# Row statistics as 128x4 columns spread over PSUM by TensorE, norm pieces in PSUM, the sums of squares on GpSimd, the last FFN pair ahead of the last two down products, and one key slab for two

## The chip, the cores and the metric

The kernel runs on one NeuronCore of one Trainium2 chip. The metric is device microseconds of one execution, the median of several runs. The core has five engines with queues of their own: PE (TensorE, matmuls; PEld is its weight load), DVE (VectorE), ACT (ScalarE), POOL (GpSimd) and SP (SyncE, which here only issues DMAs). They meet only through semaphores.

## The reference, cut to what matters

Two blocks in a row over one stream x of 1024 positions by 1024 channels, all in float32.

```
# first block
h = rmsnorm(x) ; z = h @ w_in                       # 1024 x 2560
y_a = a_bg * dwconv3(a_cg * a_h)
u   = dwconv31(b_val * sigmoid(b_gate)) + bias
y_b = silu(layernorm(u))                            # mean and variance over 512 channels
x   = x + [y_a, y_b] @ w_out
h = rmsnorm(x)
x = x + (silu(dwconv3(h @ w_gate)) * (h @ w_up)) @ w_down      # D_FF = 2816 = 22 tiles of 128
x = rmsnorm(x, norm_final_g)
# second block
h = rmsnorm(x) * (1 + scale) + shift ; pooling mixer, 4 groups ; x = x + gate * (... @ a_w_out)
hk = rmsnorm(x) * (1 + scale_kv) + shift_kv ; k, v = hk @ w_kv # 2 kv heads of 64: k is 128 columns, v 128
h = rmsnorm(x) * (1 + scale) + shift ; q, z = h @ b_w_in ; windowed attention with sinks
x = x + gate * (o * silu(z)) @ b_w_out
out = rmsnorm(x, final_g)
```

## The kernel before, in words

**Layout.** Channels lie on the 128 partitions and positions on the free axis: the stream `X` is 128 x 8 x 1024. Every product is in two parts, a high one rounded to fp32r and a low rest: w_hi\*x_hi + w_hi\*x_lo + w_lo\*x_hi, three matmuls of 128x512 (lines 449 to 451, and 502 to 504 in `gated_pair`). A weight **slab** is 128x1024. SP brings it to one of two `w_raw` buffers (L326), ACT rounds it to `w_hi` (L807, `weight_hi`), POOL makes `w_lo` (L356, `lower`), and the next slab but one can only be loaded when POOL is done with that buffer (`slab_ready`). Six pairs of `w_hi`/`w_lo` places are reused in a planned order (`SLAB_PLACE`, `slab_ends`, `refill_after`).

**Order.** Each engine's program is written out by hand; nothing is scheduled by a planner. PE takes *slab tiles* (24 matmuls: one 128-column slab against one half of the positions) and *down jobs* (16 tiles of 6 matmuls, whose results DVE adds to `X`: L1375, L1280, L1282, L1688), rotating through PSUM banks 0 to 3. A tile waits until the reader of its bank, four tiles back, is done (`freed`).

**Norms.** There are seven: MIX, FFN, FIN1 and POOL (both on the stream after the FFN), KV and ATT (one statistic for both), FIN2. Behind each of the 16 adds of the last down job ACT squares the new piece of `X` into one of two buffers (L828), and the squares are summed over the 8 channel tiles of a half into `T[2]`: on DVE (`add_square`, L1209) for FFN, KV and the second half of FIN2, on POOL (`sums`, L380) for FIN1 and the first half of FIN2. For POOL, DVE sums squares that carry FIN1's gain (L1523) and joins the two sums (L1529). A float32 matmul with a 128x128 matrix of ones (`stat`, L466) sums over partitions and leaves 128 equal rows of 512. ACT takes the root (L851), DVE the reciprocal (`rstd`, L1198), both on 128x512. Then for each of 16 pieces DVE multiplies (`scaled`, L1222, from `X` and `T[2]`, both in SBUF, into a piece in SBUF), ACT rounds it into `norm_hi` (`hi`, L859 or L861) and DVE subtracts (`low`, L1231 or L1233). PE follows piece by piece in `gated_pair`, 6 matmuls for each. `apply_early` puts the first pieces behind the last adds of the down job, `apply` does the rest.

**The layernorm** of the first block sits inside the four output down jobs. In front of tile 4 of the first one PE sums the four conv results of each half with eight matmuls of ones (L552); DVE subtracts the mean, ACT squares, POOL sums (L406), PE sums again (L558), ACT takes the root, DVE the reciprocal (L1388, 128x512), DVE scales (L1395), ACT applies SiLU and rounds, DVE subtracts (L1400). Those steps are placed behind single adds by `behind_first` and `behind_second`.

**FFN.** Eleven pairs: pair 0 in `gated_pair`, ten loop turns with two pairs and one down job of two y tiles each, and after the loop the pair for y tile 21 and the last down job. `ffn_y` has two places.

**Keys.** Slabs 150 and 151 each hold the 64 key columns of one kv head twice, slab 152 the values. `gated_pair` computes both key slabs, then two slab tiles give the values (in the KV norm's `norm_hi`), and only then may ACT write the ATT norm over it.

## Time and profile before

| | us |
|---|---|
| median of 3 runs (2251.2 to 2256.27) | 2255.36 |
| the profiled execution, its own time | 2253.53 |
| its span, first to last instruction | 2251.6 |
| PE busy in the span | 2125.0 (94%) |
| DVE busy | 1340.2 (60%) |
| ACT busy | 657.6 (29%) |
| POOL busy | 612.6 (27%) |
| mean granted TensorE clock | 0.98 |

The page gives busy time by engine, the span in 40 slices, the chain that ended last and the costliest groups. PE's busy time is that of overlapping matmuls, so it tells that PE had work and not that it was at its peak. What ended an idle time stands behind an arrow: `[8.46 <-DVE norm_lo L1233]` says that the engine had stood still for 8.46 us and that the DVE instruction of line 1233 released it.

### The profile page before, as it was taken

The numbers are of one execution on the slowest core, as the hardware profiler recorded it, in microseconds if no ns is written. First come the engines' busy times: TensorE is split into PE (matmuls) and PEld (weight loads), VectorE is DVE, ScalarE is ACT, GpSimd is POOL, SyncE is SP. The second block draws the span as 40 slices with busy tenths as digits, with TensorE's granted clock in tenths as the row PEclk, the third lists the DMA queues.
The fourth block names the chain that finished last, engine by engine and source line by source line (L and its number), as shares of the span: only waits on it lengthen the run. The fifth ranks groups of instructions, "written<-read, shape, count | busy, mean of one in ns | idle before, by whom it ended". The sixth has DMA issues, their size and how long they took to land.

```text
span 2251.6 us, 24476 instructions
## 1 busy us (share of the span) xinstructions
PE 2125.0 (94%) x9252; PEld 1704.7 (76%) x9252; DVE 1340.2 (60%) x1652; ACT 657.6 (29%) x1150; POOL 612.6 (27%) x280
## 2 busy tenths in 40 slices
PE   6999988899999999999889999999999789779996
PEld 4788766788888888888668888888888568557885
DVE  6998878455545556554785452463553831995557
ACT  4222333321222212121442122121221432785112
POOL 2223420321212222121431132121221123443622
PEclk9999999999999999999989999999999999999998
DMA  4131110422323231232011121111111111010202
GB/s 143 57 96 46 56 38 0 178 65 85 112 93 112 94 111 50 99 105 100 19 56 38 38 70 43 38 56 47 47 56 31 45 47 38 10 29 10 75 10 75
DMA packets 42951, 141.70 MB, mean 63 GB/s; under 512 B 3568, under 2 KB 7808, under 8 KB 42880
## 3 DMA queue, kind: packets, MB, share of 16 engines
q1 hardware_dynamic: 29984, 101.38, 14.2%
q10 hardware_dynamic: 12896, 39.36, 4.6%
q8 instruction: 47, 0.77, 0.1%
q14 instruction: 24, 0.20, 0.0%
HBM read 136.50 MB, written 7.36 MB: 64 GB/s over the span
## 4 chain that ended last, share of the span: by engine, by line
PE 81%; DVE 14%; issue 2%; ACT 1%; POOL 1%; DMA 1%; DVEq 0%; ACTq 0%; SPq 0%; POOLq 0%
PE psum L449 26%; PE psum L451 26%; PE psum L450 26%; DVE temp L1222 2%; DVE temp L1198 1%; DVE top L1635 1%; DVE w_lo L1653 1%; DVE probs L1632 1%; DVE norm_lo L1233 1%; PE psum L459 1%; DVE temp L1209 1%; DVE norm_lo L1231 1%; POOL w_lo L356 1%; DMA w_raw<-in_slabs 0%; DVE stream L1269 0%
## 5 line engine op out<-in xcount | busy, mean ns | idle before, releaser
L356 POOL TENSOR_TENSOR w_lo<-w_raw,w_hi 128x1024 fp32r<-128x1024 f32 x177 | 451.4, 2568 | 1347.5 <-ACT w_hi L807 1345.8
L449 PE MATMUL psum<-norm_hi,w_hi 128*128 128x512 f32 x1712 | 670.3, 392 | 19.0 <-ACT keys L884 6.5
L450 PE MATMUL psum<-norm_lo,w_hi 128*128 128x512 f32 x1712 | 668.6, 391 | 0.0
L451 PE MATMUL psum<-norm_hi,w_lo 128*128 128x512 f32 x1712 | 668.5, 390 | 0.0
L449 PEld LDWEIGHTS psum<-norm_hi,w_hi 128*128 128x128 f32 x1712 | 323.1, 189 | 88.4 <-issue 19.4
L451 PEld LDWEIGHTS psum<-norm_hi,w_lo 128*128 128x128 f32 x1712 | 322.8, 189 | 67.8
L450 PEld LDWEIGHTS psum<-norm_lo,w_hi 128*128 128x128 f32 x1712 | 323.0, 189 | 67.2
L884 ACT ACTIVATE temp<-psum 128x512 f32<-128x512 f32 x160 | 93.8, 598 | 460.7 <-PE psum L451 445.1
L1282 DVE SCALAR_TENSOR_TENSOR stream<-psum,mods,stream 128x512 f32<-128x512 f32 x160 | 119.7, 750 | 170.8 <-PE psum L451 170.6
L807 ACT CAST w_hi<-w_raw 128x1024 fp32r<-128x1024 f32 x158 | 158.8, 1046 | 146.0 <-DMA w_raw<-in_slabs 81.3
L1280 DVE TENSOR_TENSOR stream<-psum,stream 128x512 f32<-128x512 f32 x176 | 118.2, 688 | 79.4 <-PE psum L451 79.1
L1334 DVE SCALAR_TENSOR_TENSOR psum<-glu,vec,psum 128x1024 f32<-128x1024 f32 x116 | 149.6, 1290 | 3.9
L449 PE MATMUL psum<-ffn_y_hi,w_hi 128*128 128x512 f32 x352 | 141.4, 402 | 1.5 <-DVE stream L1280 1.4
L450 PE MATMUL psum<-ffn_y_lo,w_hi 128*128 128x512 f32 x352 | 139.2, 396 | 0.0
L451 PE MATMUL psum<-ffn_y_hi,w_lo 128*128 128x512 f32 x352 | 139.2, 395 | 0.0
L1469 DVE CUSTOM_DVE_ANT_0 ada_raw<-ada_raw,c_act 128x1024 f32<-128x1024 f32 x64 | 117.3, 1891 | 1.6 <-ACT c_act L985 1.6
L1442 DVE TENSOR_SCALAR psum<-temp,vec 128x1024 f32<-128x1024 f32 x22 | 28.3, 1288 | 142.7 <-ACT temp L884 142.4
L502 PE MATMUL psum<-norm_hi,w_hi 128*128 128x512 f32 x160 | 71.0, 444 | 38.8 <-DVE norm_lo L1233 18.2
L1564 DVE TENSOR_TENSOR temp<-temp 128x1024 f32<-128x1024 f32 x40 | 73.7, 1843 | 49.5 <-ACT temp L884 48.4
L449 PE MATMUL psum<-pool_y_hi,w_hi 128*128 128x512 f32 x256 | 101.5, 397 | 0.0
L451 PE MATMUL psum<-pool_y_hi,w_lo 128*128 128x512 f32 x256 | 101.1, 395 | 0.0
L450 PE MATMUL psum<-pool_y_lo,w_hi 128*128 128x512 f32 x256 | 101.1, 395 | 0.0
(171 smaller groups left out, 2865.2 us busy)
## 6 DMA issues: line engine op xcount, KB each, us to landing
w_raw<-in_slabs SPq DMA_DIRECT2D x177, 512.0 KB, 3.5
ada_raw<-in_ada ACTq DMA_DIRECT2D x10, 3072.0 KB, 12.2
stream<-in_x SPq DMA_DIRECT2D x8, 512.0 KB, 8.7
out<-stream SPq DMA_DIRECT2D x8, 512.0 KB, 2.8
skew_scratch<-row_scratch ACTq DMA_DIRECT2D x1, 3072.0 KB, 18.0
ada_raw<-in_ada ACTq DMA_DIRECT2D x1, 2048.0 KB, 9.8
bias<-skew_scratch ACTq DMA_DIRECT2D x4, 512.0 KB, 3.7
c_act<-in_c ACTq DMA_DIRECT2D x1, 512.0 KB, 11.4
```

What stands on the lines that cost most here:

```text
L356: nc.gpsimd.tensor_tensor(WL[place][:, :], RAW[at % 2][:, :], WH[place][:, :].bitcast(f32), ALU.subtract).then_inc(slab_ready, 1)
L449: nc.tensor.matmul(dst, wh, xh, start=n == 0, stop=False)
L450: nc.tensor.matmul(dst, wh, xl, start=False, stop=False)
L451: last = nc.tensor.matmul(dst, wl, xh, start=False, stop=n == len(terms) - 1)
L502: nc.tensor.matmul(dst, wh, xh, start=k == 0, stop=False)
L807: nc.scalar.copy(WH[place][:, :], RAW[at % 2][:, :]).then_inc(w_hi_done, 1)
L884: nc.scalar.activation(dst, bank[b], func, scale=scale).then_inc(act_read, 1)
L1280: ins = nc.vector.tensor_tensor(part, src, part, ALU.add)
L1282: ins = nc.vector.scalar_tensor_tensor(part, src, mods[:, gate + e:gate + e + 1], part, ALU.mult, ALU.add)
L1334: step(nc.vector.scalar_tensor_tensor(ACC, window, w, ACC, ALU.mult, ALU.add))
L1469: ins = nc.vector.tensor_tensor_reduce(out=ADA[:, n, :], in0=ADA[:, n, :], in1=c_act[:, :], scale=1.0, scalar=0.0, op0=ALU.mult, op1=ALU.a ...
L1564: step(nc.vector.tensor_tensor(body(T[dst]), body(T[src]), T[src][:, 16 - width:16 - width + S], ALU.add))
```

## The change

- **Statistics.** `stat` no longer makes 128 equal rows. `columns` takes the summed squares as the stationary operand, 128 positions at a time, and a single column of ones as the moving one: 4 matmuls leave 128x4. ACT's root and DVE's reciprocal work on 128x4 (`stat_col`). `across` then multiplies each column, broadcast over 128, by the identity: 4 matmuls put the 128 equal rows of 512 into a PSUM bank (`spread`). `stat` stands in front of tile 11 of the down job (before: 10, for POOL 13), `spread` in front of tile 13. For the second half they stand at steps 4 and 7 of `gated_pair`. MIX stays as it was.
- **Pieces.** `scaled` reads the spread statistic from bank 4 or 5 and writes its piece to bank 6 or 7, from which ACT and DVE read it.
- **Sums.** FFN, KV and FIN2 (all but the very last square) are summed on POOL. For POOL, DVE multiplies FIN1's plain squares by the squared gain and accumulates in PSUM (`add_gained`); ACT's second square of each piece goes, and `join_sums` becomes a second term of the column matmuls.
- **Layernorm.** POOL adds up the four conv results of each half in `T[2]` (6 adds, counted by `ln_pre`) behind its third weight slab of the last in-projection, and PE sums with one matmul of ones for each half in front of tile 4. Variance, root, reciprocal and spread go the new way, and DVE's scale and low steps are laid one behind each add.
- **FFN.** `ffn_y` has three places. The pair for y tile 21 comes straight behind the last turn's two pairs, ahead of the last two down jobs; SP loads the slabs in that order.
- **Keys.** Slab 150 holds the 64 key columns of both heads, brought by two DMAs of 64 columns in a row; slab 151 the values. `gated_pair` computes both, the two separate value tiles are gone, ACT makes the doubled keys with four copies of 64 partitions for each half, and writes the ATT norm of a half as soon as it has read that half.
- **End.** 14 of the 16 final pieces are normed by DVE (before 13), the other 2 by ACT and POOL; POOL's factor is a second spread in bank 7, copied to SBUF by ACT.

The diff, cut to its core:

```diff
-SLAB_PLACE += [0, 1] + [4]
-SLAB_PLACE += [2 * p + h for p in (1, 0, 2, 0, 2, 0, 1, 2, 0, 1, 2, 0) for h in (0, 1)]
+SLAB_PLACE += [0, 1]
+SLAB_PLACE += [2 * p + h for p in (1, 2, 0, 2, 0, 2, 1, 0, 2, 1, 0, 2) for h in (0, 1)]
...
         def piece(n, m):
-            return body(T[1], m % 2) if n != ATT and m < 8 else slot(m)
+            if n != MIX:
+                return bank[6 + m % 2]
+            return body(T[1], m % 2) if m < 8 else slot(m)
...
# sync
+            load_slabs(2, LAST_GATE)
+            load_slabs(LAST_GATE, LAST_GATE + 2, 2)
+            load_slabs(LAST_GATE + 2, LAST_GATE + 4, -2)
+            load_slabs(LAST_GATE + 4, ATT_SLAB)
+            sp.wait_ge(slab_ready, ATT_SLAB - 1)
+            for n in range(2):
+                if n:
+                    sp.wait_ge(keys_ready, 16)
+                keys = slab_in[ATT_SLAB + n, :, :].rearrange("p (k c) -> p k c", k=KT)[:, :, HD * n:HD * n + HD]
...
# gpsimd
                 lows(14 + 3 * j, 17 + 3 * j)
+                if j == MT - 1:
+                    gp.wait_ge(taps_done, MT)
+                    for n in range(1, MT):
+                        gp.wait_ge(conv_done, n + 1)
+                        for half in range(2):
+                            part = body(T[2], half)
+                            if n > 1:
+                                gp.wait_ge(ln_pre, 2 * n - 3 + half)
+                            nc.gpsimd.tensor_tensor(part, body(UB[4], half) if n == 1 else part,
+                                                    body(UB[(n + 4) % 5], half), ALU.add).then_inc(ln_pre, 1)
...
-            lows(26, FFN_SLAB + 6)
+            lows(26, FFN_SLAB + 2)
+            sums(FFN)
+            lows(FFN_SLAB + 2, FFN_SLAB + 6)
...
-            lows(ATT_SLAB - 8, ATT_SLAB + 8)
+            lows(ATT_SLAB - 8, ATT_SLAB + 2)
+            sums(KV)
+            lows(ATT_SLAB + 2, ATT_SLAB + 8)
...
# tensor
+            def columns(dst, terms):
+                for b in range(4):
+                    for n, (summed, weight) in enumerate(terms):
+                        last = nc.tensor.matmul(dst[:, b:b + 1], summed[:, P * b:P * b + P], weight[:, 0:1],
+                                                start=n == 0, stop=n == len(terms) - 1)
+                return last
+            def across(dst, half):
+                for b in range(4):
+                    last = nc.tensor.matmul(dst[:, P * b:P * b + P], stat_col[:, half, b:b + 1].to_broadcast([P, P]),
+                                            ident[:, :], start=True, stop=True)
+                return last
+            def spread(n, half):
+                pe.wait_ge(rstd_done, 2 * STATS_BEFORE[n] + half + 1)
+                across(stat_bank(n, half), half).then_inc(spread_done, 1)
...
                 if (n, m) == (0, 4):
-                    pe.wait_ge(conv_done, MT)
                     for half in range(2):
-                        for j in range(MT):
-                            last = nc.tensor.matmul(bank[4 + half], ones[:, :], body(UB[(j + 4) % 5], half),
-                                                    start=j == 0, stop=j == MT - 1)
-                        last.then_inc(ln_sum, 1)
-                if (n, m) in ((0, 12), (1, 2)):
+                        pe.wait_ge(ln_pre, 2 * MT - 3 + half)
+                        nc.tensor.matmul(bank[4 + half], ones[:, :], body(T[2], half), start=True, stop=True
+                                         ).then_inc(ln_sum, 1)
+                if (n, m) in ((0, 11), (0, 15)):
+                    half = m // 15
+                    pe.wait_ge(ln_added, 3 * half + 3)
+                    columns(bank[4 + half], [(body(T[2], half), ones)]).then_inc(ln_var, 1)
+                if (n, m) in ((0, 14), (1, 2)):
                     half = n
...
-            t, g = POOL_TILE - 20, POOL_SLAB - 4
-            pair_job(t, g, SLAB_PLACE[g], 124, [(dve_read, 224)], crossed=False)
+            ffn_pairs(FFN_LOOPS - 1)
+            t, g = POOL_TILE - 36, LAST_GATE
+            pair_job(t, g, SLAB_PLACE[g], 124, [(act_read, 124)], crossed=False)
+            pe.wait_ge(f_lo, FT - 2)
+            down_job(t + 4, g + 2, SLAB_PLACE[g + 2], 208, [(act_read, 128)], FYH[:, 0:3:2, :], FYL[:, 0:3:2, :])
...
             gated_pair(t, g, KV, [(dve_read, 400)])
-            pe.wait_ge(slab_ready, g + 3)
-            for half in range(2):
-                pe.wait_ge(act_read, 192 + 4 + half - 3)
-                slab_tile(t + 4 + half, SLAB_PLACE[g + 2], half)
...
# scalar, keys
             for half in range(2):
+                act.wait_ge(tiles, t + 2 * half + 1)
                 for n in range(2):
-                    read_tile(t + 2 * half + n, KD[n][:, hs(half)])
...
+                    for side in range(2):
+                        ins = nc.scalar.copy(KD[n][HD * side:HD * side + HD, hs(half)],
+                                             bank[(t + 2 * half) % 4][HD * n:HD * n + HD, :])
+                ins.then_inc(act_read, 1)
+                read_tile(t + 2 * half + 1, VT[:, hs(half)])
+                for m in range(8 * half, 8 * half + 8):
+                    hi(ATT, m)
+                if half == 0:
+                    weight_his(ATT_SLAB + 5, ATT_SLAB + 6)
...
# vector
-                nc.vector.scalar_tensor_tensor(piece(n, m), X[:, k, hs(half)], gain(n, k), body(T[2], half),
+                nc.vector.scalar_tensor_tensor(piece(n, m), X[:, k, hs(half)], gain(n, k),
+                                               body(T[2], half) if n == MIX else bank[4 + half],
                                                ALU.mult, ALU.mult).then_inc(norm_done, 1)
...
             def behind_last(j):
-                if j >= 2:
-                    add_gained(j - 2)
+                if j:
+                    add_gained(j - 1)
                 if j == 10:
-                    join_sums(0)
-                if j == 14:
                     rstd(POOL, 0)
-
+                if j >= 13:
+                    scaled(POOL, j - 13)
+                if j >= 14:
+                    low(POOL, j - 14)
```

## Rows read from the trace of the kernel before

**Rows 1.** The page: busy time by engine, and the granted clock in 40 slices.
```profile
PE 2125.0 (94%) x9252; PEld 1704.7 (76%) x9252; DVE 1340.2 (60%) x1652; ACT 657.6 (29%) x1150; POOL 612.6 (27%) x280
...
PEclk9999999999999999999989999999999999999998
```

**Rows 2.** Waits of PE: releaser, us in total, times, longest.
```profile
PE psum L502 <- DVE norm_lo L1233: 18.2, 6, 8.5
PE psum L502 <- DVE norm_lo L1231: 15.1, 6, 6.5
...
PE psum L449 <- DVE stream L1375: 6.3, 3, 3.8
```

**Rows 3.** Stretches: length, busy us of PE, PEld, DVE, ACT, POOL, then PEclk.
```profile
500.00:550.00 50.00, 50.00 (x219) 40.66 (x218) 26.04 (x28) 9.88 (x13) 13.77 (x6) 1.00 0.33 115
...
323.70:329.70 6.00, 5.95 (x14) 4.69 (x15) 2.90 (x5) 0.00 (x0) 0.00 (x0) 0.51 0.01 5
```

**Rows 4.** Groups of DVE by form: busy us, mean ns of one.
```profile
L1282 DVE SCALAR_TENSOR_TENSOR stream<-psum,mods,stream 128x512 f32<-128x512 f32 x160 | 119.7, 750 | 170.8 <-PE psum L451 170.6
...
L1198 DVE RECIPROCAL temp<-temp 128x512 f32<-128x512 f32 x10 | 33.5, 3346 | 11.7 <-ACT temp L851 11.7
...
L1445 DVE SCALAR_TENSOR_TENSOR psum<-temp,vec,psum 128x1024 f32<-128x1024 f32 x22 | 28.4, 1290 | 3.0 <-DVE psum L1442 1.5
...
L1209 DVE TENSOR_TENSOR temp<-temp 128x512 f32<-128x512 f32 x35 | 23.8, 681 | 1.9 <-ACT temp L828 1.5
...
L1648 DVE RECIPROCAL total<-total 128x4 f32<-128x4 f32 x32 | 5.7, 178 | 1.1
```

**Rows 5.** Groups of POOL: a sum of two 128x512 tiles.
```profile
L406 POOL TENSOR_TENSOR temp<-temp 128x512 f32<-128x512 f32 x6 | 7.8, 1306 | 5.4 <-ACT temp L945 4.8
```

**Rows 6.** Time line of the layernorm: PE's sums, POOL's third slab, an add of job 3.
```profile
263.34 7.03 PE L552 MATMUL psum<-glu,ones 128*128 128x512 f32 x16
...
266.95 2.35 POOL L356 TENSOR_TENSOR w_lo<-w_raw,w_hi 128x1024 fp32r<-128x1024 f32 x1 [2.21 <-ACT w_hi L807]
...
344.99 0.69 DVE L1375 TENSOR_TENSOR stream<-psum,stream 128x512 f32<-128x512 f32 x1 [0.81 <-PE psum L451]
```

**Rows 7.** Time line behind the FFN norm: ACT's late slabs, PE's restart.
```profile
401.97 1.04 ACT L807 CAST w_hi<-w_raw 128x1024 fp32r<-128x1024 f32 x1 [5.16 <-DMA w_raw<-in_slabs]
...
406.37 0.79 PE L449 MATMUL psum<-norm_hi,w_hi 128*128 128x512 f32 x1 [6.22 <-ACT temp L884]
```

**Rows 8.** Time line around the POOL norm, in order of time.
```profile
1108.38 1.19 DVE L1523 TENSOR_TENSOR temp<-temp,squares_gained 128x512 f32<-128x512 f32 x1
...
1130.28 0.76 PE L502 MATMUL psum<-norm_hi,w_hi 128*128 128x512 f32 x1 [8.46 <-DVE norm_lo L1233]
...
1149.59 1.05 ACT L807 CAST w_hi<-w_raw 128x1024 fp32r<-128x1024 f32 x1 [0.78 <-DMA w_raw<-in_slabs]
...
1164.44 0.60 ACT L884 ACTIVATE temp<-psum 128x512 f32<-128x512 f32 x1 [2.53 <-PE psum L504]
```

**Rows 9.** Time line from the KV norm's end to the second query pair.
```profile
1790.61 0.72 ACT L861 ACTIVATE norm_hi<-temp,mods 128x512 fp32r<-128x512 f32 x1 [0.60 <-DVE temp L1222]
...
1799.40 1.04 ACT L807 CAST w_hi<-w_raw 128x1024 fp32r<-128x1024 f32 x1 [5.67 <-DMA w_raw<-in_slabs]
...
1801.09 0.77 PE L449 MATMUL psum<-norm_hi,w_hi 128*128 128x512 f32 x1 [6.52 <-ACT keys L884]
...
1815.84 0.47 PE L502 MATMUL psum<-norm_hi,w_hi 128*128 128x512 f32 x1 [2.17 <-DVE norm_lo L1233]
...
1843.27 0.77 PE L449 MATMUL psum<-norm_hi,w_hi 128*128 128x512 f32 x1 [5.41 <-ACT q_then_o L884]
```

**Rows 10.** Time line: four float32 transposes on PE, eight records.
```profile
1889.37 1.03 PE L696 MATMUL psum<-ident,probs 128*128 128x128 f32 x8
```

**Rows 11.** Time line of the end.
```profile
2233.91 1.79 PE L466 MATMUL psum<-temp,ones 128*128 128x512 f32 x2 [2.77 <-DVE temp L1209]
...
2239.85 6.42 DVE L1269 SCALAR_TENSOR_TENSOR stream<-stream,vec,temp 128x512 f32<-128x512 f32 x5
```

More of the change, by code:

```diff
@@ L84, in slab_ends @@
     products(2)
-    for _ in range(FFN_LOOPS):
+    for _ in range(FFN_LOOPS - 1):
         products(2), products(2), down()
-    products(2, False), down()
+    products(2), products(2), products(2, False), down(), down()
     for _ in range(GROUPS):
@@ L97, in slab_ends @@
         ends.extend(downs + [t, t])
[L98 removed]
+    products(2), products(2)
     products(6, False)
@@ L461, in stat @@
                     return
[L462 to L467 removed]
+                sums = 14 * SUMS_BEFORE[FIN1 if n == POOL else n] + 7 * half + 7
+                if n == FIN2 and half:
+                    pe.wait_ge(sum_done, sums - 1)
+                    pe.wait_ge(square_done, 16 * SUMS_BEFORE[FIN2] + 16)
+                    terms = [(sum_place(n, half), ones), (squares(n, 15), ones)]
+                elif n == POOL:
+                    pe.wait_ge(sum_done, sums)
+                    pe.wait_ge(gained_sum, 8 * half + 8)
+                    terms = [(body(T[2], half), ones), (SUM_PLAIN[:, hs(half)], eps)]
+                else:
+                    pe.wait_ge(sum_done, sums)
+                    terms = [(sum_place(n, half), ones)]
+                columns(stat_bank(n, half), terms).then_inc(stat_done, 1)
+            def columns(dst, terms):
[12 more added lines that the diff above has]
+                across(stat_bank(n, half), half).then_inc(spread_done, 1)
             def slab_tile(t, place, half, at=None):
@@ L492, in gated_pair @@
                     for k in range(KT):
-                        if half == 0 and k == 3 and norm != ATT:
+                        if half == 0 and norm == MIX and k == 3:
                             stat(norm, 1)
-                        if half == 0 and norm == POOL and k in (5, 6):
-                            stat(FIN1, k - 5)
+                        if half == 0 and norm not in (MIX, ATT):
+                            if k == 4:
+                                stat(norm, 1)
+                            if k == 7:
+                                spread(norm, 1)
                         pe.wait_ge(lo_done, APPLIED_BEFORE[norm] + 8 * half + k + 1)
@@ L526, in down_job @@
                         between(j)
-                    if norm is not None and j == (13 if norm == POOL else 10):
+                    if norm is not None and j == 11:
                         stat(norm, 0)
+                    if norm is not None and j == 13:
+                        spread(norm, 0)
                     freed(j, dve_read, own_base, before)
@@ L618, in pool_turn @@
                     gated_pair(0, g, POOL, [(dve_read, d)])
+                    for half in range(2):
+                        stat(FIN1, half)
                     pe.wait_ge(slab_ready, g + 3)
@@ L623, in pool_turn @@
                     input_slab(3, 6, act_read, a + 3)
+                    for half in range(2):
+                        spread(FIN1, half)
                 else:
@@ L795, in _ @@
             stat(FIN2, 1)
+            spread(FIN2, 1)
+            across(bank[7], 1).then_inc(spread_done, 1)
         @block.scalar
@@ L1009, in _ @@
                 read_tile(t + 2 + half, body(T[1], half))
+            for half in range(2):
                 act.wait_ge(f_mul, FT + half)
-                nc.scalar.copy(FYH[:, 1, hs(half)], bank[6 + half]).then_inc(f_hi, 1)
+                act.wait_ge(tiles, POOL_TILE - 32 + 8 * half + 8)
+                nc.scalar.copy(FYH[:, 2, hs(half)], bank[6 + half]).then_inc(f_hi, 1)
             weight_his(POOL_SLAB, POOL_SLAB + 2)
@@ L1181, in _ @@
                                      ).then_inc(stream_gained, 1)
+            last_gain(14)
             mean_root(FIN2, 1)
+            last_gain(15)
+            act.wait_ge(spread_done, spreads(FIN2, 1) + 1)
+            nc.scalar.copy(body(T[2], 1), bank[7]).then_inc(rstd_copied, 1)
         @block.vector
@@ L1245, in apply @@
                     scaled(n, m)
+                    if m == 7 and n not in (MIX, ATT):
+                        rstd(n, 1)
                     if m:
@@ L1577, in _ @@
                                             ).then_inc(p_lo, 1)
-                    if g == 0 and n < 2:
-                        rstd(FIN1, n)
-                    elif g == 0:
+                    if g == 0 and n == 0:
+                        for half in range(2):
+                            rstd(FIN1, half)
+                    elif g == 0 and n > 1:
                         for m in range(8 * (n - 2), 8 * (n - 2) + 8):
```

322 lines of the change are left out of this document (161 added, 161 removed).

## The prediction, made before the kernel was built

> **What bounds the kernel now.** The page first: PE has work for 94% of the span, DVE for 60%, and the granted clock is full but for two dips in 40 slices [rows 1]. So time is either PE's work, or one of few stretches in which PE stands still. A stretch without waits gives the price of work: 219 matmuls in 50 us, 0.228 us each. A slab tile of 24 is 5.5 us, a down tile or a step of `gated_pair` (6) is 1.4 us [rows 3]. The list of PE's waits names the stretches: 33 us for the low parts of norm pieces (L1233, L1231) and 6.3 us in the layernorm's down jobs [rows 2]; the time lines add 6.2 us behind the FFN norm [rows 7], and 6.5 and 5.4 us around the keys and queries [rows 9]. A wait has a tail: after the longest of the 6.3 us the clock was 0.51, that is 1.2 GHz, and 14 matmuls took 6.0 us where 3.2 would do [rows 3]. I book 3 us for such a tail. Everything that the change moves off DVE outside these stretches is free already.
>
> **Prices of the new pieces.** A column statistic and a spread are each four small float32 matmuls (eight records). Nearest row: four transposes of 128 columns, 1.03 us with the last one's latency [rows 10]; I take 0.9, between 0.5 (one column moves instead of 128) and 1.8 at half clock. The two-term one for POOL: 1.8. A reciprocal falls from 3.35 to 0.18 us, and it is paid ten times outside the layernorm and FIN1 [rows 4]. `scaled` and `low` on a PSUM piece: DVE with a PSUM input and SBUF output takes 0.750 us, with a PSUM input and output 1.290 for twice the width, 0.65 for 512 [rows 4]; I take 0.75 and 0.65, as now, so DVE's step stays at some 1.35 us against PE's 1.4. The Trainium skill's table (VectorE: DVE Perf Modes, the section on the TRN2 errata) gives PSUM-to-SBUF operations 62 cycles more of fixed cost than SBUF-to-SBUF ones; by it I estimate 0.06 us more per instruction, a step of about 1.47 us, and for 64 pieces some 5 us less gain. The rows show no such surcharge.
>
> **Layernorm: +5 us.** POOL ends its third slab at 266.95 + 2.35 = 269.3 [rows 6], and only then makes the six sums of two, 1.31 us each [rows 5]. The first half needs five of them: 275.9; the second 277.2. PE wants them in front of tile 4, at 263.3, where before it began eight matmuls of ones that took 7.0 us [rows 6]. With one such matmul for each half (7.03 / 8 = 0.9) it goes on at about 279 instead of 270: +9, and +3 for a half-clock tail after 12.6 us of standing. Back come the 6.3 us of waits [rows 2] and their 3 us tail, since one DVE step now lies behind each add. Two ones matmuls (1.8) become two statistics and two spreads (3.6), and the first spread waits some 1.2 us, as ACT makes all eight squares before the first root. 9 + 3 - 6.3 - 3 + 1.8 + 1.2 = 5.7, taken as 5. In this stretch the wait is new: behind PE's stand all later tiles, and behind POOL's six sums its last two `mix_y_lo`, not needed before job 1.
>
> **FFN norm: -5 us.** It starts from job 3's first add [rows 6]. Off DVE: two reciprocals, 6.3 us net, and the sums behind tile 10, seven at 0.68, 4.8 us [rows 4]; the first-half sums were hidden. Back: DVE waits 1.6 us for the first spread (tiles 11 and 12 go first), PE pays 0.9 + 0.9 in `gated_pair`, DVE waits 1.3 for the second, and then PE's 1.4 limits instead of DVE, about 1. POOL's sums at 1.31 us keep up with tiles of 1.4 [rows 5, 3]. What is late next is the same as now: ACT rounds four slabs only behind its last piece, the last two wait for DMAs, and PE restarts after that [rows 7]. This chain of some 11 us moves with the norm, and PE will stand in front of it for 9 us rather than 6.2.
>
> **The last FFN pair: nothing by itself.** PE's work is the same in another order; the pair's conv hides under the first of the two down jobs (16 x 1.4 us), so the last down starts when it did, with DVE free.
>
> **POOL norm: -8 us.** DVE's gained sums took 1.19 us beside POOL's own, instead of 0.68 [rows 8, 4]. In PSUM they have one SBUF input, like the adds; eight of them save 4 us ahead of the first statistic. The reciprocal saves 3.2, the join about 1, and `scaled`/`low` now begin behind tiles 13 and 14: 3. So PE starts at 1119.3 instead of 1130.28 [rows 8]. It doesn't keep this: ACT rounds slabs 98 and 99 between two pieces, the second waits for a DMA that follows POOL's low part of slab 97 [rows 8], and I expect PE to stand 4 us there. End of the pair at 1153 instead of 1164.4 [rows 8]; FIN1's two statistics now follow it (1.8), its two spreads a little later (1.8).
>
> **KV norm: -5 us**, as FFN. **Keys and ATT: -15 us.** From ACT's last KV piece (1791.3) to the query pair (1843.3) it took 52 us [rows 9]. New: the same three slabs, to 1800.4, 9.1 us; four key copies and the value, 0.5 each (at most 0.72 [rows 9]), 2.6; one piece, 1.4; then the pair, 16 x 1.4 = 22.4 us, with 2.5 us between the halves, where ACT rounds a slab and reads the other half. 38 us: 14 less, of which 48 x 0.228 = 10.9 is the two tiles that are gone. The 5.4 us wait and its tail go (-3), a tail behind the 11 us that PE now stands ahead of ATT comes (+2). The two key DMAs in a row are costed at nothing: they lie in the last pooling turn, ahead of a down job of 22 us; without that cover each costs up to the 5.7 us that ACT waited for a slab [rows 9]. The identity on POOL at the start: nothing, POOL is idle.
>
> **FIN2: -3.5 us.** DVE ended at 2239.85 + 6.42 = 2246.3 [rows 11]. The last statistic starts as before, at 2233.9, two terms at low clock 2 us, root and reciprocal 0.4, spread 1.7, six products at 0.75: 2242.6. The second spread, ACT's copy and two products on POOL end there too. The last DMA follows as before.
>
> **Sum.** 5 - 5 - 8 - 5 - 15 - 3.5 = -31.5. The profiled execution took 2253.5 (its span 2251.6), 1.8 under the median: 2222 against it, **2224 as a median**.
>
> **Rivals.**
> *The gains are half eaten.* Every new wait ties three engines; if each of the ten round trips costs 1 us more and the layernorm's stand is 3 us longer, 2237. For it: PE is in order, nothing fills its stand. Against: two down tiles lie between statistic and spread.
> *The norms don't get shorter.* The change doesn't do what it is said to do, since round trips replace what leaves DVE: FFN, POOL and KV at 0, so -13.5, 2242. For it: 6.2 us behind FFN are ACT's slabs, not DVE. Against: the 8.5 us at POOL are DVE's.
> *More gain.* POOL's sums ahead of tile 4 come sooner, small matmuls cost 0.5, fewer half-clock tails (two fewer, -6): -42, 2213.
> *Slower: PSUM pieces.* `scaled` and `low` get slower, and PE follows DVE through 64 pieces. It decides from a step of 1.4 + 31.5 / 64 = 1.9 us on. If an instruction that meets another engine on its PSUM bank takes 1.19 instead of 0.68, as L1523 did beside POOL [rows 8, 4], a step is 2.4 us: +64, 2288. Against: L1282 and L1445 use PSUM beside PE without it [rows 4].
>
> **Chances.** Forecast 0.62; half eaten 0.15; norms no shorter 0.05; more gain 0.12; slower 0.06. Within 0.2% (4.5 us, about what a measurement of this kernel can tell from nothing) 0.02. Faster 0.92, slower 0.06. The range takes the two middle rivals and the bound on the small matmuls (about 30 of them, +-0.4 us): 2209 to 2243.
>
> **What would show it.** PE standing some 12 us in front of tile 4 of the first output job, released by POOL; no wait in jobs 1 to 3; 9 us ahead of the second FFN pair, with ACT's slabs behind it; a 4 us stand inside the POOL pair; 11 us ahead of ATT and none ahead of query pair 1; reciprocals of 0.2 us; steps of 1.35 us on DVE. I am wrong if PE waits long for `spread`'s reciprocals, if L1222 or L1233 exceed 0.8 us, or if POOL's sums fall behind the down tiles.

## The result, and the profile of the changed kernel

The changed kernel takes **2224.25 us** (median of 4 runs, 2223.68 to 2224.98), the kernel before beside it 2255.82 us (4 runs). The ratio is 0.9865, 95% interval 0.9853 to 0.9877: faster by 31.6 us. The forecast was 2224.0, with a range of 2209 to 2243.

The page of the changed kernel, the lines that answer to [rows 1]:

```profile
span 2221.9 us, 24671 instructions
...
PE 2115.9 (95%) x9392; PEld 1709.6 (77%) x9392; DVE 1265.5 (57%) x1619; ACT 644.5 (29%) x1138; POOL 653.0 (29%) x317
...
PEclk9999899999999999999999999999999999999999
```

PE is busy for 9.1 us less and the span is 29.7 us shorter, so 20.6 us of the gain are time in which PE stood still. Its list of waits, against [rows 2], shows which stands went and which came:

```profile
PE psum L497 <- DVE w_lo L1764: 28.7, 27, 2.9
PE psum L580 <- DVE norm_lo L1335: 18.8, 9, 10.1
PE psum L580 <- DVE norm_lo L1333: 15.0, 6, 6.5
PE psum L631 <- POOL temp L442: 11.7, 1, 11.7
PE psum L497 <- ACT temp L976: 9.3, 2, 8.4
PE psum L507 <- ACT glu L918: 6.2, 1, 6.2
PE psum L528 <- POOL temp L415: 4.3, 4, 2.6
```

The first lies in attention and the sixth ahead of the changed parts; both were there before (28.0 and 6.3 us). The 6.3 us behind L1375 are gone; the 11.7 us behind POOL's six sums are new; the 8.4 us behind ACT are the restart behind the FFN norm; the 10.1 us stand ahead of ATT.

**Stage by stage.** I compare the same event in both traces: before, after, and what the stage between two such marks changed.

| up to | before | after | stage | booked |
|---|---|---|---|---|
| first add of output job 3 | 344.99 | 347.57 | +2.6 | +5 |
| PE's restart behind the FFN norm | 406.37 | 404.34 | -4.6 | -5 |
| ACT's last read in the first gate group of pooling | 1208.58 | 1202.83 | -3.7 | -8 |
| last KV piece on ACT | 1790.61 | 1780.22 | -4.6 | -5 |
| first 128x4 reciprocal of attention | 1904.95 | 1878.52 | -16.0 | -15 |
| last one | 2047.17 | 2020.14 | -0.6 | 0 |
| end of the span | 2251.6 | 2221.9 | -2.7 | -3.5 |

The sum is -29.7 in the traces, -31.5 booked. The medians differ by 31.6 because the profiled run of before was 2.3 us under its median and that of after 0.6 under.

**The layernorm.** Time lines of POOL and PE, against [rows 6] (start, duration, in brackets the idle time before):

```profile
266.83 2.35 POOL L391 TENSOR_TENSOR w_lo<-w_raw,w_hi 128x1024 fp32r<-128x1024 f32 x1 [1.99 <-ACT w_hi L904]
269.13 2.48 POOL L442 TENSOR_TENSOR temp<-glu 128x512 f32<-128x512 f32 x2
271.57 4.92 POOL L442 TENSOR_TENSOR temp<-temp,glu 128x512 f32<-128x512 f32 x4
...
275.32 1.22 PE L631 MATMUL psum<-temp,ones 128*128 128x512 f32 x1 [11.71 <-POOL temp L442]
...
347.57 0.69 DVE L1477 TENSOR_TENSOR stream<-psum,stream 128x512 f32<-128x512 f32 x1 [0.81 <-PE psum L499]
```
```profile
276.00:278.00 2.00, 2.00 (x3) 0.50 0.00 0
278.00:280.00 2.00, 2.00 (x5) 0.54 0.00 0
280.00:282.00 2.00, 2.00 (x10) 1.00 0.00 0
```

PE stands from 263.6 to 275.3, released by the fifth sum, as forecast, and works at half the clock until nearly 280. Counted by the starts of PE's down tiles, it is 9.1 us later than before behind the stand and its tail, and 12.4 us behind the statistics and spreads (tile 4 of job 1 starts at 306.67 instead of 294.32). By job 3 it has won back 9.8 of them.

**The restart behind the FFN norm**, against [rows 7]. ACT and PE, then stretches (length, PE busy, granted clock):

```profile
400.09 1.04 ACT L904 CAST w_hi<-w_raw 128x1024 fp32r<-128x1024 f32 x1 [5.30 <-DMA w_raw<-in_slabs]
...
404.34 0.79 PE L497 MATMUL psum<-norm_hi,w_hi 128*128 128x512 f32 x1 [8.37 <-ACT temp L976]
```
```profile
396.00:404.00 8.00, 0.00 (x0) 0.71 0.45 137
404.00:410.00 6.00, 5.66 (x14) 0.54 0.99 380
410.00:416.00 6.00, 6.00 (x28) 1.00 0.55 223
```

The norm is shorter, and PE stands longer for ACT's slabs. Half the matmuls of full clock in the 6 us behind the stand, 14 instead of 28, are its tail: by this count 14 x 0.228 = 3.2 us.

**The POOL norm**, against [rows 8]: POOL's first sum, PE at the first statistic, at the first gated matmul, at piece 10, and behind the FIN1 statistics:

```profile
1090.89 4.78 POOL L391 TENSOR_TENSOR w_lo<-w_raw,w_hi 128x1024 fp32r<-128x1024 f32 x2 [39.41 <-ACT w_hi L904]
1095.64 1.31 POOL L415 TENSOR_TENSOR ada_raw<-temp 128x512 f32<-128x512 f32 x1
...
1107.00 0.27 PE L528 MATMUL psum<-ones,temp 128*128 128x1 f32 x1 [2.42 <-POOL ada_raw L415]
...
1120.51 0.47 PE L580 MATMUL psum<-norm_hi,w_hi 128*128 128x512 f32 x1 [2.01 <-DVE norm_lo L1335]
...
1142.87 0.50 PE L580 MATMUL psum<-norm_hi,w_hi 128*128 128x512 f32 x1 [2.54 <-DVE norm_lo L1335]
...
1155.56 0.47 PE L497 MATMUL psum<-norm_hi,w_hi 128*128 128x512 f32 x1 [0.93 <-ACT temp L976]
```
```profile
1109.00:1112.00 3.00, 3.00 (x9) 0.55 0.00 0
1120.00:1123.00 3.00, 1.60 (x6) 1.00 0.00 0
1142.00:1148.00 6.00, 5.13 (x15) 0.72 0.50 175
1157.00:1160.00 3.00, 3.00 (x9) 0.51 0.00 0
```

Three small waits, of 2.4, 2.5 and 0.9 us, have a stretch at a lower granted clock close behind them: nine matmuls in 3 us, where 15 stand at full clock, and 15 in 6 us instead of 26. The wait of 2.0 us at 1120.51 has none (clock 1.00), nor has one of 1.05 us at 1137.35. So a low stretch behind a wait doesn't yet show that the wait caused it.

**DVE and POOL by form**, against [rows 4, 5]:

```profile
L1323 DVE SCALAR_TENSOR_TENSOR psum<-stream,gains,psum 128x512 f32<-128x512 f32 x48 | 35.9, 754 | 8.6 <-PE psum L535 7.3
L1335 DVE SCALAR_TENSOR_TENSOR norm_lo<-psum,mods,norm_hi 128x512 fp32r<-128x512 f32 x48 | 35.7, 746 | 15.5 <-ACT norm_hi L952 14.9
L1323 DVE SCALAR_TENSOR_TENSOR temp<-stream,vec,temp 128x512 f32<-128x512 f32 x16 | 18.2, 1147 | 0.4
...
L1333 DVE TENSOR_TENSOR norm_lo<-temp,norm_hi 128x512 fp32r<-128x512 f32 x16 | 11.0, 685 | 9.1 <-ACT norm_hi L950 8.9
L1333 DVE TENSOR_TENSOR norm_lo<-psum,norm_hi 128x512 fp32r<-128x512 f32 x16 | 10.9, 684 | 0.1
...
L1309 DVE RECIPROCAL stat_column<-stat_column 128x4 f32<-128x4 f32 x10 | 1.6, 172 | 8.3 <-ACT stat_column L943 8.2
```
```profile
L415 POOL TENSOR_TENSOR temp<-temp 128x512 f32<-128x512 f32 x41 | 53.2, 1297 | 78.6 <-ACT temp L927 76.0
```

The subtraction takes as long from PSUM as from SBUF (684 and 685 ns); the product with both tiles in SBUF, in the first norm, takes 1147 ns in the mean against 754 (three of the sixteen take 2.9 us each, the others 0.75: see the last section); a reciprocal of columns takes 0.17 us.

### The profile page after: what moved, and what is told of

It reads as the page before. It is cut to its first block, busy times and chain, and to the rows that moved or that the text cites. A ratio compares the mean times of both kernels' runs of the same rounds, so it can differ in the third digit from the quotient of the medians.

```text
span 2221.9 us, 24671 instructions
## 1 busy us (share of the span) xinstructions
PE 2115.9 (95%) x9392; PEld 1709.6 (77%) x9392; DVE 1265.5 (57%) x1619; ACT 644.5 (29%) x1138; POOL 653.0 (29%) x317
## 4 chain that ended last, share of the span: by engine, by line
PE 84%; DVE 9%; POOL 3%; ACT 2%; issue 1%; DMA 1%; ACTq 0%; POOLq 0%; SPq 0%; DVEq 0%
PE psum L497 27%; PE psum L499 27%; PE psum L498 26%; POOL temp L415 1%; DVE w_lo L1764 1%; DVE top L1746 1%; DVE probs L1743 1%; POOL w_lo L391 1%; DVE psum L1323 1%; PE psum L580 1%; PE psum L507 1%; PE psum L582 1%; PE psum L581 1%; DVE norm_lo L1335 1%; DVE temp L1323 1%
## 5 line engine op out<-in xcount | busy, mean ns | idle before, releaser
L497 PE MATMUL psum<-norm_hi,w_hi 128*128 128x512 f32 x1696 | 662.9, 391 | 10.1 <-ACT temp L976 9.3
L498 PE MATMUL psum<-norm_lo,w_hi 128*128 128x512 f32 x1696 | 661.9, 390 | 0.0
L499 PE MATMUL psum<-norm_hi,w_lo 128*128 128x512 f32 x1696 | 661.3, 390 | 0.0
L580 PE MATMUL psum<-norm_hi,w_hi 128*128 128x512 f32 x160 | 68.6, 429 | 33.8 <-DVE norm_lo L1335 18.8
## 6 DMA issues: line engine op xcount, KB each, us to landing
ada_raw<-in_ada ACTq DMA_DIRECT2D x10, 3072.0 KB, 12.6
```

Source lines behind the costliest of these rows:

```text
L497: nc.tensor.matmul(dst, wh, xh, start=n == 0, stop=False)
L498: nc.tensor.matmul(dst, wh, xl, start=False, stop=False)
L499: last = nc.tensor.matmul(dst, wl, xh, start=False, stop=n == len(terms) - 1)
L580: nc.tensor.matmul(dst, wh, xh, start=k == 0, stop=False)
```

## The experiments

Twelve kernels. Beside each lay new runs of the kernel before; its median was 2255.36, 2254.61, 2255.03 and 2254.60 us in the four groups of runs. The intervals of the ratios are some 0.0015 to either side, 3 us; where an effect is smaller I give the marks of the trace beside it. Differences are taken to the changed kernel's 2224.25. A stage in the trace ends at the marks of the table above; "in the FFN loop" compares the same cast of `ffn_y_hi` in two traces.

### Single parts, alone or undone

**key_slab_alone**: the kernel before with the key part only.
```diff
-SLAB_PLACE += [0, 1] + [4]
+SLAB_PLACE += [0, 1]
...
-                    read_tile(t + 2 * half + n, KD[n][:, hs(half)])
+                    for side in range(2):
+                        ins = nc.scalar.copy(KD[n][HD * side:HD * side + HD, hs(half)],
+                                             bank[(t + 2 * half) % 4][HD * n:HD * n + HD, :])
```


> The kernel before with only the key slab of the change: one slab that holds both key heads, four copies that double them, ATT pieces read between the halves; every norm as before. My theory: the key part is worth 15 us by itself, of which 48 matmuls at 0.228 us are 10.9 and the rest is the stand and tail ahead of the query pair; the trace after showed 16.0 us less in this stage. So 2241 us, ratio 0.993 (0.9925 to 0.9945). Rival: the part beyond the two tiles needs the pieces in PSUM, so only 10.9 us: 2245, ratio 0.995.

Measured 2236.8 us against 2255.36, ratio 0.9925 (0.9908 to 0.9942): 18.6 us in the medians where I expected 15, and 16.4 between the spans of the two traces. In the trace the stage from the last KV piece (1791.18) to attention's first reciprocal (1888.76) is 16.8 us shorter than before, and 16.0 us shorter in the changed kernel. So over half of the change's gain is this part, and it doesn't need the PSUM pieces: the rival fell.

**sums_dve**: `sums(FFN)` and `sums(KV)` off POOL, `add_square` on DVE as before.
```diff
-            sums(FFN)
...
+                if 2 <= j <= 8:
+                    add_square(n, j - 1)
...
+                if j >= 10:
+                    add_square(n, j - 1)
```


> The changed kernel with the sums of squares of the FFN and KV norms back on DVE, the rest as changed. My theory: these sums are the main part of the gain of those two norms, seven of them of 0.68 us behind tile 10 in each, so +4.8 us each, 2234 us (ratio 0.9905). Rival: DVE has room there because the statistic waits on PE and ACT anyway: no change, 2224 (ratio 0.986).

Measured 2227.42 us, +3.2, ratio 0.9881 (0.9864 to 0.9897). The trace is 3.2 us behind the changed kernel's in the FFN loop, and its KV stage is 1.9 us longer. It wins 1.6 us back in the POOL norm, since a stretch at low clock is missing there that has nothing to do with the sums (see fin1_roots). Both theories were off: moving the sums is worth 2 to 3 us a norm. In the FFN norm one of the seven sums falls where DVE waited anyway (362.88), and the other six cost 0.6 us each from start to start; the second reciprocal comes at 381.60 instead of 378.25.

**full_stats**: at FFN and KV one matmul of ones over 512 columns, root and reciprocal in place in PSUM.
```diff
+                if n in (FFN, KV):
+                    nc.tensor.matmul(stat_bank(n, half), ones[:, :], sum_place(n, half), start=True, stop=True
+                                     ).then_inc(stat_done, 1)
+                    return
                 columns(stat_bank(n, half), terms).then_inc(stat_done, 1)
...
```


> The changed kernel with full 128x512 statistics at the FFN and KV norms: one matmul of ones over 512 columns, root and reciprocal (3.35 us instead of 0.18) in place in PSUM, no spread. My theory: the columns bring only some 1 us per norm net, since the spreads' round trips (DVE waited 1.6 and 2.8 us for them) and 1.6 us of PE's small matmuls give back what the reciprocal saves: 2226 us (2225 to 2228), ratio 0.987. Rival: the short reciprocals are what shortened the norms, 4 x 3.2 us come back: 2237, ratio 0.992.

Measured 2224.9 us, +0.7, ratio 0.9876 (0.986 to 0.9893): the same. The trace is 0.2 us behind in the FFN loop, and its KV stage is 1.3 us longer. The group that makes it telling:

```profile
L1319 DVE RECIPROCAL psum<-psum 128x512 f32<-128x512 f32 x4 | 13.5, 3364 | 3.3 <-ACT psum L951 3.3
```

DVE pays 12.8 us more for four reciprocals, and the kernel 0.7. The column form, the change's most visible idea, brings next to nothing at these two norms. In the changed kernel DVE waits 1.60 and 2.77 us for the two spreads of the FFN norm (366.61 and 382.46), and these round trips give back what the short reciprocals save. At the other norms it was not taken back alone.

**pieces_sbuf**: 48 of 64 pieces in SBUF again.
```diff
-            if n != MIX:
+            if n == ATT:
                 return bank[6 + m % 2]
```


> The changed kernel with the pieces of the FFN, POOL and KV norms in SBUF again (48 of 64 pieces), the rest as changed. My theory: where a piece lies does not matter to the time, the instructions take 0.75 and 0.68 us from either: 2224 us within 1.5. Rival A, by the Trainium skill's table of PSUM surcharges (0.06 us per instruction): SBUF is faster, 96 instructions, up to 5 us less, 2219. Rival B: beside the sums on POOL, instructions of DVE whose inputs and output all lie in SBUF are slowed, as the 1.19 us of the gained sums before and the 1.15 us of the first norm's pieces: 10 instructions in each norm at 0.4 us, 4 to 12 us more, 2228 to 2236.

Measured 2225.81 us, +1.6, ratio 0.9873 (0.9857 to 0.9889): at the edge of my theory's bound, and its runs (2224.35 to 2228.69) overlap those of the changed kernel. The trace is 0.1 us ahead in the FFN loop, and the stages of POOL and KV are 0.9 and 1.6 us longer. In the POOL stage the low clock at 1157 is missing again; up to the third statistic the norm had lost 2.6 us. That is a mild form of rival B:

```profile
L1335 DVE SCALAR_TENSOR_TENSOR norm_lo<-temp,mods,norm_hi 128x512 fp32r<-128x512 f32 x32 | 26.6, 834 | 3.1 <-ACT norm_hi L952 2.5
...
L1323 DVE SCALAR_TENSOR_TENSOR psum<-stream,gains,psum 128x512 f32<-128x512 f32 x16 | 12.0, 755 | 0.6
```

The low part of an SBUF piece takes 834 ns in the mean instead of 746. The theory that the place doesn't matter holds for the time within its noise, not for the instructions. Rival A, SBUF as the faster place, fell.

**pair_undone**: the last FFN pair between the last two down jobs again.
```diff
-    for _ in range(FFN_LOOPS - 1):
+    for _ in range(FFN_LOOPS):
         products(2), products(2), down()
-    products(2), products(2), products(2, False), down(), down()
+    products(2, False), down()
...
```


> The changed kernel with the order of the last FFN pair undone: both down jobs of turn 9 and the last one where they were before, the last pair between them, its gating behind the pair. My theory, the prediction's term of nothing by itself, corrected by one step: ACT rounds slabs 94 and 95 behind the last gating, and POOL's sums start behind their low parts, 1.4 us later counted from the start of the last down job than in the changed kernel: 1.5 us more, 2226 us, ratio 0.9872. Rival A: nothing, 2224. Rival B: DVE's late adds (three in a row before) and its gained sums collide, the POOL norm starts 4 us later: 2228, ratio 0.988.

Measured 2227.04 us, +2.8, ratio 0.9873 (0.9857 to 0.9888); its runs (2223.89 to 2228.67) overlap those of the changed kernel, so the marks have to tell. The last down job starts at 1089.0 in both traces. POOL's first sum starts at 1097.00 instead of 1095.64, the 1.4 us expected, and PE reaches the first statistic 1.3 us later. But the low clock now falls on the statistic's own small matmuls (0.56 us a record pair instead of 0.36), and the first gated matmul is at 1123.46, 2.95 us later. These last 1.6 us can't be put down to the order: in all_five, which has the changed kernel's order, the low clock falls on the same small matmuls and costs the same 1.6 us. So "nothing by itself" was wrong by the 1.4 us of POOL's later start, and by up to 3 us if the low clock belongs to it.

### What the stands that are left are worth

**ln_ones**: PE sums the glu tiles again, the rest of the layernorm stays changed.
```diff
+                    pe.wait_ge(conv_done, MT)
                     for half in range(2):
-                        pe.wait_ge(ln_pre, 2 * MT - 3 + half)
-                        nc.tensor.matmul(bank[4 + half], ones[:, :], body(T[2], half), start=True, stop=True
-                                         ).then_inc(ln_sum, 1)
+                        for j in range(MT):
+                            last = nc.tensor.matmul(bank[4 + half], ones[:, :], body(UB[(j + 4) % 5], half),
+                                                    start=j == 0, stop=j == MT - 1)
+                        last.then_inc(ln_sum, 1)
...
```
The rest of the diff takes the six sums out of POOL's program.


> The changed kernel with one part of the layernorm undone: the sums of the glu tiles are made by PE again, eight matmuls of ones in front of tile 4 of the first output job, instead of six sums on POOL and two matmuls. My theory: PE's 11.7 us stand in front of tile 4 is this part's price; with the matmuls PE goes on at about 270.6 instead of 279, and the columns, spreads and new order of the jobs keep their gain: 8 us less, 2216 us, ratio 0.9825. Rival: what comes sooner waits in jobs 1 to 3, as 6.3 us did before the change, since DVE and ACT have the same work behind the sums: 2 us less, 2222, ratio 0.985.

Measured **2214.38 us**, -9.9, ratio 0.9821 (0.9806 to 0.9836). PE's row in its time line, and the stretch behind it:

```profile
262.78 7.03 PE L622 MATMUL psum<-glu,ones 128*128 128x512 f32 x16
```
```profile
270.00:276.00 6.00, 6.00 (x28) 1.00 0.20 76
```

Job 3's first add is at 337.88, 9.7 us sooner than in the changed kernel, and 7.1 sooner than before. The waits of 6.3 us don't return, so the rival fell: the spreads and DVE's new order are the good part of the layernorm's change, POOL's sums the bad one.

**ffn_reads**: ACT reads the first pair's tiles ahead of slab 32.
```diff
-            weight_his(30, 34)
-            act.wait_ge(tiles, FFN_TILE)
+            weight_his(30, 32)
+
+            def late_loads():
+                weight_his(32, 34)
+                act.wait_ge(tiles, FFN_TILE)
...
-            ffn_tile(0, FFN_TILE, FFN_TILE, False, 0, FFN_TILE)
+            ffn_tile(0, FFN_TILE, FFN_TILE, False, 0, FFN_TILE, late_loads)
```


> The changed kernel with ACT reading the four tiles of the first FFN pair behind slab 31 instead of slab 33, and the two small loads on ACT's queue behind that. My theory: the 8.4 us that PE stands ahead of the second FFN pair are ACT's order: the tiles are ready at 396 us and ACT waits 5.3 us for a slab's DMA before it reads them. PE then goes on when POOL has slab 31's low part, 398.7 instead of 404.3: 5.6 us less, 2218.5 us, ratio 0.9835. Rival: the DMAs of slabs 32 and 33 are the bound, and PE stands behind tile 2 of the second pair instead: at most 1 us less, 2223.5, ratio 0.9855.

Measured **2213.9 us**, -10.3, ratio 0.9821 (0.9806 to 0.9836). The restart, and the stretches that answer to those above:

```profile
396.99 0.49 PE L497 MATMUL psum<-norm_hi,w_hi 128*128 128x512 f32 x1 [0.47 <-POOL w_lo L391]
```
```profile
396.00:404.00 8.00, 7.53 (x34) 1.00 0.38 133
404.00:410.00 6.00, 6.00 (x28) 1.00 0.98 367
```

The restart is 7.35 us sooner, since PE starts on slab 30 before slab 31's low part is there, and in the FFN loop it is 9.7 us ahead (a cast of `ffn_y_hi` at 490.02 instead of 499.73). The 2.4 us between are the tail, which I had left out of the expectation; the count of matmuls above gave 3.2. The trace also lacks the low clock of the next experiment.

**fin1_roots** and **pool_slabs**, two orders on ACT in the POOL norm:
```diff
-            for half in range(2):
-                mean_root(FIN1, half)
...
+                    if first_turn and n == 0:
+                        for half in range(2):
+                            mean_root(FIN1, half)
```


> The changed kernel with ACT's two roots of the third statistic (FIN1) behind its first two reads of the gated pair instead of ahead of them. My theory: PE's 0.93 us stand behind these statistics goes, and with it the dip of the clock to 0.51 from 1157 to 1160 us that costs 1.5 us: 2.4 us less, 2222 us, ratio 0.985. Rival: the dip comes from the eight small matmuls, whose engine time is nearly empty, and stays: 0.9 us less, 2223.3.


```diff
-                if m in (7, 9):
-                    weight_his(POOL_SLAB + m - 5, POOL_SLAB + m - 3)
+                if m in (7, 15):
+                    weight_his(POOL_SLAB + (2 if m == 7 else 4), POOL_SLAB + (4 if m == 7 else 6))
```


> The changed kernel with ACT rounding slabs 98 and 99 behind the last piece of the POOL norm instead of behind piece 9. My theory: the 2.5 us stand inside the pair at 1142 us and the dip of the clock to 0.70 behind it (1.8 us) go: 4.3 us less, 2220 us, ratio 0.984. Rival: the slabs of the first pooling turn come later by the same, and PE stands ahead of slab 98 or 100 instead: no change, 2224.

2222.37 us (-1.9, ratio 0.9855, 0.984 to 0.987) and 2218.93 us (-5.3, ratio 0.9847, 0.9833 to 0.986). In the first, the stretch from 1157 to 1160 has clock 1.00 and 15 matmuls instead of 0.51 and 9, although the eight small statistic matmuls stand where they stood. That looks like my theory, but other traces speak against it. The 0.93 us stand is in nine traces, and the low clock behind it only in four: after, full_stats, ln_ones and pair_undone. In sums_dve, pieces_sbuf, ffn_reads, pool_slabs and key_slab_order the stand is there and the clock behind it is 1.00. The last of these is edited only some 600 us later:

```profile
1155.66 0.47 PE L497 MATMUL psum<-norm_hi,w_hi 128*128 128x512 f32 x1 [0.93 <-ACT temp L976]
```
```profile
1157.00:1160.00 3.00, 3.00 (x15) 1.00 0.00 0
```

Each of the five is 1.6 us faster than the changed kernel's trace from the third statistic to the first gate group by this alone. So the roots' order is worth the stand, 1.1 of the 2.7 us that this stretch is shorter in fin1_roots; what brings the low clock is open. In pool_slabs, 1142 to 1148 holds 26 matmuls at clock 1.00 instead of 15 at 0.72. This low stretch does go with its stand: it is in all nine traces that have a stand there, of 2.3 to 3.9 us, and in none of the three without one. Stand and tail give 4.0 us in the trace, near the 4.3 expected; the rest of the 5.3 may be the low clock at 1157, which is missing here too.

**key_slab_order**: the keys and two ATT pieces ahead of slab 154 on ACT.
```diff
-            weight_his(ATT_SLAB + 2, ATT_SLAB + 5)
+            weight_his(ATT_SLAB + 2, ATT_SLAB + 4)
...
+                    if m == 1:
+                        weight_his(ATT_SLAB + 4, ATT_SLAB + 5)
```


> The changed kernel with ACT reading the keys and the first two ATT pieces ahead of the cast of slab 154, for whose DMA it waits 5.2 us, instead of behind it. My theory: of PE's 10.1 us stand ahead of ATT only the last 2 us are ACT's and DVE's order (the slab's low part is ready at 1792.0, the first piece at 1794.0): 2 us less, 2222 us, ratio 0.985. Rival: the slab is the whole bound and the pieces hide behind it: no change, 2224.

Measured **2217.18 us**, -7.1, ratio 0.9831 (0.9818 to 0.9845). The stand ahead of ATT:

```profile
1786.21 0.76 PE L580 MATMUL psum<-norm_hi,w_hi 128*128 128x512 f32 x1 [3.79 <-DVE norm_lo L1337]
```

It was 10.08 us in the changed kernel. Both theories fell: ATT reads slabs 152 and 153, and slab 154, for which ACT waited 5.2 us, belongs to the query pair behind it. So 6.3 of the 10.1 us were ACT's order; behind the remaining 3.8 stand the key copies and the first pieces on ACT. From the last KV piece to attention's first reciprocal the trace is 5.75 us shorter; the rest of the 7.1 may again be the low clock at 1157.

**all_five** is these five edits together, **all_six** adds one on POOL:
```diff
+            sums(FIN1, (f_lo, FT + 1), last=8)
             lows(POOL_SLAB, POOL_SLAB + 2)
-            sums(FIN1, (f_lo, FT + 1))
+            sums(FIN1, first=8)
```


> The changed kernel with the five edits together: matmuls of ones for the glu sums, ACT's reads of the first FFN pair ahead of slab 32, the third statistic's roots behind two reads, slabs 98 and 99 behind the last POOL piece, keys read ahead of slab 154. My theory: they lie in five stretches that do not touch, so the single effects add: 9.9 + 10.3 + 1.9 + 5.3 + 2 = 29 us less than the changed kernel, 2195 us, ratio 0.973. Rival: two edits that serve the same wait (roots and slabs in the POOL norm) give only the larger one, 2 us less of it: 2197.

> The kernel of the five edits, and POOL makes the first seven sums of the third statistic ahead of the low parts of slabs 94 and 95 instead of behind them. My theory: the POOL norm's first statistic waits for POOL, not for DVE: its sums start at 1095.6 behind 4.8 us of low parts, though the squares are there 2.3 us sooner. PE's 2.4 us wait at this statistic goes, and the dip of the clock to 0.55 behind it (1.4 us): 3.8 us less than with the five edits, 2192 us, ratio 0.972. Rival: DVE's own sums, one per tile, end as late, and the low parts push the second half's sums: no change, 2196.

**2195.95 us** (ratio 0.9735, 0.9722 to 0.9748) and **2192.21 us** (ratio 0.9723, 0.971 to 0.9736). The sum of the five single medians is 9.9 + 10.3 + 1.9 + 5.3 + 7.1 = 34.5 us; together they gave 28.3. The 29 that I expected came out because the keys stood in it with 2 us, so the agreement is luck. For the 6 us between the traces give two reasons. The low clock at 1157, 1.6 us, is missing in the traces of four of the five single edits, and together it can be missing only once. And in all_five the low clock behind POOL's first statistic costs 1.6 us more than in the changed kernel. Only one execution of each kernel has a trace, so how much of the medians this explains is open; the 3 us uncertainty of each is the other candidate.

The sixth edit took 3.7 us, as expected in size. PE's wait for POOL's `ada_raw` fell from 2.4 to 0.4 us, but the low clock behind the statistic stayed, where I had expected it to go:

```profile
1088.00:1091.00 3.00, 3.00 (x9) 0.50 0.59 175
```

The other 1.6 us are those by which it is shorter again than in all_five.

In all_six PE is busy for 97% of the span:

```profile
PE 2119.0 (97%) x9404; PEld 1711.6 (78%) x9404; DVE 1276.2 (58%) x1619; ACT 645.5 (29%) x1138; POOL 647.8 (30%) x311
```

## Why the prediction was right, and where it was not

For the keys, the largest term, and for FFN, KV and FIN2 both mechanism and size were right; for the POOL norm the mechanism was incomplete. That the total came out within 0.3 us of the median is luck: in the traces two terms are off by 2.4 and 4.3 us with opposite signs, and the spans differ by 29.7 us where 31.5 were booked.

- **Layernorm, +5.** Right in kind and place (12.6 us of stand booked, 11.7 measured), too dear by 2.4. The part that was mis-sized is the stand with its tail: by the starts of its tiles PE was 9.1 us late, not 9 + 3, since tile 4 began at 278.1 instead of 269.8 and the low clock cost 0.8 us more, not 3. The others held: statistics, spreads and their wait added 3.2 us (1.8 + 1.2 booked), and 9.8 came back (6.3 + 3 booked).
- **FFN norm, -5.** Right (-4.6). The restart behind ACT's slabs took 8.4 us, 9 booked. The split was not right: the sums were booked at 4.8 and are worth 3.2 in the trace of sums_dve (1.9 at KV), the reciprocals at 0.6 net of their round trips and are worth 0.2 in that of full_stats (1.3 at KV).
- **Last FFN pair, 0.** Wrong. The step "the last down starts when it did, with DVE free" holds, but it left out that ACT and POOL prepare slabs 94 and 95 behind the last gating, which decides when POOL's sums start. Undone, they start 1.4 us later and the kernel takes 2.8 us more; whether the low clock that makes up the rest belongs to it is open.
- **POOL norm, -8.** The term that failed: -3.7. I followed DVE's chain to a first gated matmul at 1119.3 and added no clock loss. With the 2 us by which the kernel is ahead there, it should have been at 1117.3; it was at 1120.51. POOL's chain was longer than DVE's: 4.8 us of low parts, then seven sums at one in 1.4 us, to 1106.94; with the sums first, in all_six, PE's wait is 0.4 instead of 2.4 us. The low clock behind the statistic costs another 1.4 us. The stand inside the pair, booked at 4 us, was 2.5 with a tail of 1.8 us. The pair ended 1.8 us later than worked out (the third statistic is at 1152.78, where 1153 less the 2 us gives 1151). Behind it come the 0.93 us stand and the low clock of 1.6 us, both booked at nothing; the second of them five other traces don't have.
- **KV, -5; keys and ATT, -15; FIN2, -3.5.** -4.6, -16.0 and -2.7. The keys held as worked out, with 10.1 us ahead of ATT (11 booked) and no long stand ahead of query pair 1 (0.8). What I had not seen is that 6.3 of the 10.1 us were avoidable.
- **PSUM pieces.** The rival of slower pieces fell: 754 and 684 or 746 ns an instruction. The Trainium skill's table (VectorE: DVE Perf Modes, the section on the TRN2 errata) gives a PSUM source 62 cycles more; here the subtraction takes 684 ns from PSUM and 685 from SBUF, and the kernel with SBUF pieces was not faster. The step that DVE's gained sums get shorter with one SBUF input held: 1058 and 1843 ns in the mean before, 749 after.

## What to carry to other kernels

Where PE is busy for 95% of the time, look at what each in-order engine has queued between a tile that is ready and the wait of PE: five of the six edits in the last kernel only move one block of ACT's or POOL's queue behind another, and with ln_ones they are worth 32.0 us, as much as the change itself. Price a stand at its length, and book a tail at the lower clock as a risk, not as a rule. A single trace misleads here: 1.6 us of low clock came and went between kernels that were the same up to that point, so look at several traces before you give a low stretch to an edit. And weigh the visible idea by itself: full reciprocals of 3.36 us at two norms cost this kernel 0.7 us, less than the runs can tell from nothing.

## What was unexpected of the hardware

- **The length of a stand doesn't tell whether the clock falls.** In the POOL norm a stand of 2.3 to 3.9 us inside the pair had a stretch at 0.50 (1.2 GHz) behind it in all nine traces that have it. At the first piece a stand of 2.0 us had none in eleven traces, and one of 2.55 us in pieces_sbuf had none either. The 0.93 us stand had one in four traces of nine. And in all_six the clock was 0.50 behind a stand of only 0.37 us and eight small matmuls. Length doesn't order the tails either: behind 11.7 us PE was back at full clock 4.7 us after it resumed, behind 8.4 us after 5.2.
- **Moving an operand from SBUF to PSUM made DVE faster where POOL was at work.** The low part took 834 ns in SBUF and 746 in PSUM. The Trainium skill (SBUF — State Buffer, the section on the two sides) says why this can be: a DVE instruction with two SBUF inputs and a GpSimd one that reads SBUF exclude each other. The trace agrees. The mean of 1147 ns for the first norm's product is thirteen of 0.75 us and three of 2.87 or 2.88; each of the three starts 0.1 or 0.2 us behind the start of a POOL instruction and ends 0.5 us behind its end:

```profile
46.08 2.54 POOL L391 TENSOR_TENSOR w_lo<-w_raw,w_hi 128x1024 fp32r<-128x1024 f32 x1 [3.69 <-ACT w_hi L904]
```
```profile
46.28 2.88 DVE L1323 SCALAR_TENSOR_TENSOR temp<-stream,vec,temp 128x512 f32<-128x512 f32 x1
```

In pieces_sbuf the slow low parts (1.00, 1.25, 1.26 and 2.31 us) also run beside a POOL instruction, and those recorded singly without one take 0.74 or 0.75 us. With one tile in PSUM, ten of the low parts recorded singly in the POOL and KV norms of the changed kernel ran beside POOL, and none took more than 0.75 us.
